# Two more weight slots, a two-expert loop and one block less around the expert stage of a two-layer-type transformer kernel

## The chip, the cores and the metric

The kernel runs on one NeuronCore of a Trainium2 chip. The metric is the device time of one execution in microseconds (us), median of several runs; lower is better.

## The reference, cut to what matters

`reference()` is a first block (one layer: a hybrid mixer, then a mixture of experts) followed by a second block (two layers of sparse and latent attention with a feed-forward part). The change touches the mixture of experts of the first block and the seams at its two ends:

```
def first_block(...):
    ...
    x = x + g1[:, None, :] * y                       # out1: the mixer's output projection
    h = rms_norm(x, norm2_g[l]) * (1.0 + sc2[:, None, :]) + sh2[:, None, :]
    y = moe(h, router_w[l], router_b[l], exp_w_up[l], exp_b_up[l], exp_w_down[l], exp_b_down[l])
    x = x + g2[:, None, :] * y
    ...
```

`moe` sends each of the 512 token rows to 4 of 32 experts, computes up = h @ exp_w_up + b_up, a clamped gate times a linear part, and that @ exp_w_down + b_down, weighted by the gate. All data are float32. The weights of one expert are 8 MB (up) and 4 MB (down).

## The kernel before, in words

The program is a row of stages. A stage is a *block*: each engine gets its own code, and the engines meet at the block's end. The stages here are, in order, the output projection with the routing in its tail (`out1_stage`, class `Routing`), the expert stage (`expert_stage`), and the projection of the second block.

**Weights.** An expert's weights come as 12 chunks of 1 MB (`CHUNKS`, 8 of them `UPS`). `LENT` = 22 places ("slots") in SBUF are lent to them, in turn: chunk number s (12 for each expert) lies in slot s mod 22. The pattern of slots repeats after `CYCLE` = 22 / gcd(12, 22) = 11 experts. SyncE (SP) issues every chunk, in order. In `out1_stage.loads` it issues the first 22: four before the projection's own weights, the rest when the projection is over, some of them behind a wait on a step of the routing that still uses their place. In the expert stage it waits in `load` (L2710) for the last use of the chunk that lay in the slot (`up_done`, `down_done`, L2720 to L2723), and then for the landing of the chunk four before (L2639), so that about four are under way.

**Rows.** Rows are sorted by expert into 85 groups ("row blocks") of 32, two to five for each expert. For each row block GpSimd (POOL) gathers rows with an indirect DMA (L2759) and scatters results (L2767); VectorE (DVE) transposes and scales the gathered rows (L2887, L2892, L2894), adds the bias (L2899), clamps, and multiplies; ScalarE (ACT) does the sigmoid (L2865); TensorE (PE) runs the up chunks of a row block (L2800) and then the down chunks of the row block before it (L2809). `run` is the first row block of an expert, `rest` a loop on the engine over its others.

**Loops.** PE's outer loop (L2851) holds 11 experts and runs twice, with the other experts in straight code; SP's (L2730) too. DVE's loop holds one expert, ACT's and POOL's one row block.

**Biases.** An expert's two bias rows (8 KB and 4 KB) go to `moe_bias_row`. SP issues them (L2700, L2702) in the middle of the chunks of the same expert, behind a wait on `bias_spread`, and DVE spreads them over the partitions (L2880) in the expert's first row block.

**The seam.** Between `out1_stage` and `expert_stage` all engines meet; L270 is the end of the first block. `run_idle` (L475) is a row of matmuls without use at the start of the expert stage, nine of them.

Of the kernel before, what the change touches and what calls it, by code (L numbers as in the profile page):

```python
# [254 lines left out]
def split_gemm_stage(k, name, jobs, banks=8, last_key=None, norm=None, beside=None, ready=None, wave=1, turns=0, tails=None, halved=None, loads=None, gain=None, inner=None, split_ahead=False):  # L255
# [14 lines left out]
    with ExitStack() as ctx:  # L270
# [10 lines left out]
        aside = beside and beside(ctx, evac_done)  # L281
        block = ctx.enter_context(nc.Block())
        for tail in behind:
            if tail.gpsimd:
                block.gpsimd(tail.gpsimd)
        if aside:
            block.gpsimd(aside.gpsimd)
# [6 lines left out]
        @block.sync  # L294
        def _(sp):
            if loads:
                loads(sp, behind, aside)
            else:
                if aside:
                    aside.sync(sp)  # L300
                load_chunks(k, sp, last_key)

        @block.tensor
        def _(pe):
# [73 lines left out]
            for tail in behind:  # L378
                tail.tensor_end(pe)

# [39 lines left out]
        def _(act):  # L420
# [13 lines left out]
            work(act, "act", split)  # L434

        @block.vector
        def _(dve):
# [10 lines left out]
            work(dve, "dve", split)  # L448

# [1711 lines left out]
def part1(k, a, mod_dram, h2_dram, x_dram):  # L2161
    nc = k.nc
    narrow = [P, 2, 2, ND * NARROW]
    with ExitStack() as ctx:
# [46 lines left out]
        k.expert_small, k.expert_words = tok_at + 5 * 4 * half, (w2_at - tok_at) // 4 + 8 * half  # L2211
        k.expert_w2 = nc.alloc_sbuf_tensor_at("expert_w2", [P, 8 * half], F32, offset=w2_at)
        k.split_at = w2_at + 1408
        with split_hT(k, "hT_out1"):
# [4 lines left out]
            with nc.sbuf_tensor("out1_w", narrow, F32R) as k.w_split, nc.sbuf_tensor("gated", [P, NARROW], F32) as k.gated:  # L2219
                out1_stage(k, a, tok_at, h2_dram, x_dram)  # L2220

def out1_stage(k, a, at, h2_dram, x_dram):
# [18 lines left out]
    def loads(sp, behind, aside):  # L2246
# [17 lines left out]
        load(16)  # L2264
        sp.wait_ge(routing.parted, NT)
        load(17)
        sp.wait_ge(routing.stored, 16 * NT)
        for s in (18, 19):
            load(s)
# [3 lines left out]
        load(20)  # L2273
        sp.wait_ge(routing.place_listed, 1)
        load(21)

    split_gemm_stage(k, "out1", jobs, banks=3, turns=5, tails=tails, loads=loads)


class Routing:  # L2280
# [8 lines left out]
    def __init__(self, k, ctx, at, job_bank, bank, evac_done, rank, final, h2_dram, x_dram):  # L2289
# [43 lines left out]
        self.list_bank = [b[:, 0:LISTS] for b in bank[0:2]]  # L2333
        self.squared, self.rooted, self.inverted, self.scaled, self.turned, self.taken_act, self.taken_dve = (
# [122 lines left out]
    def place(self, dve):  # L2457
# [36 lines left out]
        dve.wait_ge(self.gates_listed, 1)  # L2494
        nc.vector.tensor_copy(k.row_gate[:, 1:], self.list_bank[1])

# [7 lines left out]
    def gpsimd(self, pool):  # L2504
        k, ops = self.k, self.k.nc.gpsimd
        pool.wait_ge(self.started, 1)
        ops.tensor_scalar(k.first[:, 0:NE], self.start[0:1, :], 1.0 / BR, None, ALU.mult)
        ops.tensor_scalar(k.first[:, NE:NE + 1], self.ends[0:1, NE - 1:], 1.0 / BR, None, ALU.mult)
        ops.tensor_scalar(k.first[:, NE + 1:], self.ends[0:1, NE - 1:], 1.0 / BR, -1.0, ALU.mult, ALU.add)
# [104 lines left out]
LENT = 22  # L2614
# [25 lines left out]


def expert_stage(k, a, h2_dram, x_dram):

    nc = k.nc
    quarter = [slice(BR * q, BR * q + BR) for q in range(PARTS)]
    DOWNS, UPW = CHUNKS - UPS, 2 * YCOLS
    with ExitStack() as ctx:
        def sem(s):  # L2650
            return nc.alloc_semaphore(f"moe_{s}")

        def sb(s, shape, dt=F32):
            return ctx.enter_context(nc.sbuf_tensor(f"moe_{s}", shape, dt))

        def ps(s):
            return ctx.enter_context(nc.psum_tensor(f"moe_{s}", [P, COL], F32))

        chunk = [[k.expert_chunk(c, r) for c in range(CHUNKS)] for r in range(CYCLE)]
        loaded = k.expert_loaded  # L2660

        work = k.mod[:, 0:2, :].rearrange("p a (b n) -> p (a b) n", n=2 * P)
        rows, y, rowsT, hidT, sig, hid = (work[:, n, :] for n in range(6))
# [1129 lines left out]
```

## Time and profile before

| | |
|---|---|
| median of 3 runs | 2735.29 us (2733.44 to 2738.8) |
| the profiled execution's own time | 2732.22 us |
| its span, first to last instruction | 2730.4 us |
| PE, DVE, ACT, POOL busy | 94%, 50%, 28%, 11% of the span |
| mean DMA rate | 217 GB/s |
| mean DMA rate from 440 to 1370 us | 414 GB/s |

All times inside the span are us from its start. The expert stage lies between about 385 and 1400 us. The shares are averages over stages with different limits: what bounds the expert stage has to be read inside that window.

### The profile page before, as it was taken

What the parts mean: (1) busy time and instruction counts of PE and PEld (TensorE: products, weight loads), DVE (VectorE), ACT (ScalarE), POOL (GpSimd) and SP (SyncE); (2) the same over time, 40 slices, a digit from 0 to 9 for tenths busy, and PEclk for the clock granted to TensorE, in tenths of its full rate; (3) what the DMA queues carried; (4) which work ended last, traced back from release to release, by engine and by line L of the source; (5) the groups of instructions that cost most, each with busy time, mean ns of one, the idle gap of its engine ahead of it and who ended that gap; (6) DMA issues with size and microseconds to landing.
All of it is one profiled execution on the core that took longest, in us unless ns stands there. A gap on an engine that the chain in (4) does not pass through costs nothing. (4 is left out here: it accounts for less than half of the span.)

```text
span 2730.4 us, 56367 instructions
## 1 busy us (share of the span) xinstructions
PE 2562.3 (94%) x21559; PEld 1724.4 (63%) x21560; DVE 1356.8 (50%) x3120; ACT 755.2 (28%) x1652; POOL 299.6 (11%) x448
## 2 busy tenths in 40 slices
PE   6999989899889879999979999999999999999998
PEld 6986864344333324443448667888888766888887
DVE  3238744354434334544465785533345686544343
ACT  4236420000000000000023575422234267423322
POOL 3112002122222112222210000000000000000000
PEclk8999989999999999999989999999999999999999
DMA  7354289999999999999984201222223310122231
GB/s 231 114 191 154 78 326 379 420 419 417 417 403 420 420 417 417 379 419 419 418 285 140 94 2 39 93 93 100 93 93 104 107 44 9 62 93 101 94 107 47
DMA packets 171856, 591.15 MB, mean 217 GB/s; under 512 B 28334, under 2 KB 55790, under 8 KB 122488
## 3 DMA queue, kind: packets, MB, share of 16 engines
q1 hardware_dynamic: 159120, 565.80, 52.9%
q0 software_dynamic: 10160, 18.02, 2.0%
q10 hardware_dynamic: 2360, 4.29, 0.4%
q8 instruction: 155, 2.54, 0.4%
q14 instruction: 61, 0.50, 0.1%
HBM read 576.35 MB, written 17.45 MB: 217 GB/s over the span
## 5 line engine op out<-in xcount | busy, mean ns | idle before, releaser
L2800 PE MATMUL moe_up<-expert_w,mod 128*32 128x512 f32 x3456 | 423.8, 612 | 49.7 <-DMA expert_w<-in_exp_w_up 26.4
L2800 PEld LDWEIGHTS moe_up<-expert_w,mod 128*32 128x32 f32 x3456 | 119.7, 112 | 299.8 <-issue 222.4
L2865 ACT ACTIVATE mod<-mod 128x256 f32<-128x256 f32 x85 | 35.5, 417 | 955.7 <-DVE mod L2901 945.8
L429 ACT ACTIVATE feed_w<-ring 128x1024 fp32r<-128x1024 f32 (+1 forms) x160 | 153.8, 1035 | 263.5 <-PE feed_bank L376 263.5
L2809 PE MATMUL moe_down<-expert_w,mod 128*32 128x256 f32 x3424 | 207.9, 384 | 1.7 <-DVE mod L2912 1.7
L2800 PE MATMUL moe_up<-ring,mod 128*32 128x512 f32 x1504 | 186.1, 607 | 23.4 <-DMA ring<-in_exp_w_up 13.6
L374 PE MATMUL feed_bank<-feed_w,mlp_u_hi 128*128 128x512 f32 x512 | 199.7, 390 | 0.0
L376 PE MATMUL feed_bank<-feed_w,mlp_u_lo 128*128 128x512 f32 x512 | 199.5, 390 | 0.0
L375 PE MATMUL feed_bank<-feed_w,mlp_u_hi 128*128 128x512 f32 x512 | 199.5, 390 | 0.0
L443 DVE TENSOR_TENSOR feed_w<-ring,feed_w 128x1024 fp32r<-128x1024 f32 (+1 forms) x160 | 185.4, 1221 | 13.2 <-ACT feed_w L429 12.9
L2809 PEld LDWEIGHTS moe_down<-expert_w,mod 128*32 128x32 f32 x3424 | 121.8, 112 | 92.4 <-issue 33.8
L374 PE MATMUL feed_bank<-feed_hT_hi,feed_w 128*128 128x512 f32 x448 | 174.6, 390 | 0.0
L375 PE MATMUL feed_bank<-feed_hT_lo,feed_w 128*128 128x512 f32 x448 | 174.6, 390 | 0.0
L376 PE MATMUL feed_bank<-feed_hT_hi,feed_w 128*128 128x512 f32 x448 | 174.5, 390 | 0.0
L2136 DVE TENSOR_TENSOR x<-x,feed_bank 128x512 f32<-128x512 f32 x80 | 54.9, 687 | 229.6 <-PE feed_bank L376 229.6
L2899 DVE TENSOR_TENSOR mod<-moe_up,mod 128x512 f32<-128x512 f32 x85 | 58.0, 682 | 177.9 <-PE moe_up L2800 177.9
L3522 DVE TENSOR_TENSOR mlp_relu<-mlp_relu 128x512 f32<-128x512 f32 x64 | 44.3, 692 | 187.3 <-ACT mlp_u_hi L3519 187.3
L2800 PEld LDWEIGHTS moe_up<-ring,mod 128*32 128x32 f32 x1504 | 50.3, 111 | 132.7 <-issue 88.3
L2767 POOL DMA_INDIRECT expert_rows<-mod,moe_place x85 | 88.5, 1041 | 286.2 <-DVE mod L2922 281.7
L2887 DVE STREAM_TRANSPOSE moe_rows_turn<-mod 128x256 f32<-128x256 f32 x86 | 55.7, 648 | 111.6 <-DMA mod<-h_rows,moe_index 85.8
L1179 ACT ACTIVATE att_p<-att_p,att_neg 128x512 f32<-128x512 f32 (+3 forms) x192 | 105.3, 551 | 12.6 <-DVE att_neg L1224 12.3
L374 PEld LDWEIGHTS feed_bank<-feed_w,mlp_u_hi 128*128 128x128 f32 x512 | 96.2, 188 | 19.9
(560 smaller groups left out, 5021.6 us busy)
## 6 DMA issues: line engine op xcount, KB each, us to landing
expert_w<-in_exp_w_up SPq DMA_DIRECT2D x163, 1024.0 KB, 10.4
expert_w<-in_exp_w_down SPq DMA_DIRECT2D x81, 1024.0 KB, 10.2
ring<-in_exp_w_up SPq DMA_DIRECT2D x70, 1024.0 KB, 10.4
ring<-in_w_ff SPq DMA_DIRECT2D x32, 2048.0 KB, 8.8
ring<-in_exp_w_down SPq DMA_DIRECT2D x36, 1024.0 KB, 10.2
x<-in_exp_w_up SPq DMA_DIRECT2D x23, 1024.0 KB, 10.5
ring<-in_ada_w SPq DMA_DIRECT2D x11, 2048.0 KB, 11.0
ring<-in_w_in SPq DMA_DIRECT2D x6, 2048.0 KB, 8.3
```

The lines of the kernel that those rows point to most:

```text
L374: nc.tensor.matmul(out, lhsT.hi, rhs.hi, start=(i == 0), stop=False)
L375: nc.tensor.matmul(out, lhsT.hi, rhs.lo, start=False, stop=False)
L376: mm = nc.tensor.matmul(out, lhsT.lo, rhs.hi, start=False, stop=last)
L429: hi = nc.scalar.activation(halves.hi[:, at], w[:, at], ACT.Copy)
L443: lo = nc.vector.tensor_tensor(halves.lo[:, at], w[:, at], halves.hi[:, at].bitcast(F32), ALU.subtract)
L1179: nc.scalar.activation(p[:, b, m, 0:nk], p[:, b, m, 0:nk], ACT.Exp, bias=neg[:, b, m:m + 1], scale=-1.0, accum_out=total[:, n % 4, m:m + 1 ...
L2136: return nc.vector.tensor_tensor(k.x[:, t, cols], k.x[:, t, cols], psum, ALU.add)
L2767: pool.indirect_dma_start(y_parts, bass.IndirectOffsetOnAxis(ap=place[:], axis=0), y, None, bounds_check=NO_PLACE - 1, oob_is_err=False).t ...
L2800: mm = nc.tensor.matmul(up[quarter[q], :], rowsT[:, c, :], w[:, q], start=(c == 0), stop=(c == UPS - 1))
L2809: mm = nc.tensor.matmul(down[quarter[q], 0:YCOLS], hidT[:, 2 * at + h, :], w[:, h, q * YCOLS:(q + 1) * YCOLS], start=(at == 0 and h == 0), ...
L2887: nc.vector.transpose(turned_by_part, rows_by_run).then_inc(rows_turned, 1)
L2899: nc.vector.tensor_tensor(pre, up[:], bias_up, ALU.add).then_inc(up_taken, 1)
```

## The change

- The scratch that the chip keeps for dynamic transfers is set to 2048 bytes of a partition (it was not set before, so the default held). The room goes to `expert_w4`, two more slots: `LENT` = 24, and with it `CYCLE` = 2. `expert_chunk` maps the slots anew.
- The loops of PE and SP over experts hold 2 experts and run 15 times.
- `expert_stage` becomes the class `Experts`, whose engine code is appended to the block of the output projection through a new parameter `after` of `split_gemm_stage`. The block end between them is gone. In its place each engine waits for `first_made`, three small results of POOL. The accumulators are two of the projection's banks.
- Five chunks, not four, are issued ahead of the projection's own weights, and the waits on the routing's steps stand before other chunks.
- ACT issues the biases of expert e + 1 after those of expert e are spread; SP issues none.
- `run_idle` runs 6 matmuls, not 9. DVE zeroes `moe_bias_row` before it waits for the first gathered rows, copies the gate rows after that, and transposes the second rows before the first bias.

```diff
-def split_gemm_stage(..., split_ahead=False):
+def split_gemm_stage(..., split_ahead=False, after=None):
...
+        follower = after and after(behind[0])
         block = ctx.enter_context(nc.Block())
...
+            if follower:
+                follower.sync(sp)
...
             for tail in behind:
                 tail.tensor_end(pe)
+            if follower:
+                follower.tensor(pe)
...
-        for s in range(4):
+        for s in range(5):
             load(s)
         load_chunks(k, sp, keys[-1])
         sp.wait_ge(k.groups_done, k.last_group[k.chunk_no[keys[-1]]])
-        for s in range(4, 16):
+        for s in range(5, 17):
             load(s)
...
-LENT = 22
+LENT = 24
 CYCLE = LENT // math.gcd(CHUNKS, LENT)
...
-            def load(e, r, c0=0):
-                begin, end = first_block(sp, e - 1), first_block(sp, e)
-                for c in range(c0, CHUNKS):
-                    if c == LENT - CHUNKS:
-
-                        sp.wait_ge(bias_spread, e * 2)
-                        load_bias(sp, e)
+            def load(e, r):
+                begin = first_block(sp, e - 1)
+                for c in range(CHUNKS):
                     old = (c + CHUNKS - LENT) % CHUNKS
-                    last = begin if c < LENT - CHUNKS else end
+                    last = begin
...
-            load(1, 1, LENT - CHUNKS)
-            with sp.Fori(0, NE // CYCLE) as i:
+            with sp.Fori(0, (NE - 2) // CYCLE) as i:
                 for r in range(2, CYCLE + 2):
                     load(i * CYCLE + r, r)
-            for r in range(2, NE % CYCLE):
-                load(NE // CYCLE * CYCLE + r, r)
...
-            run_idle(k, down, 9)
+            run_idle(k, down, 6)
...
+            def next_bias(e):
+
+                act.wait_ge(bias_spread, e * 2 + 2)
+                load_bias(act, e + 1)
+
             load_bias(act, 0)
             open_gate(0)
-            with act.Fori(1, first_block(act, NE)) as b:
-                open_gate(b)
+            next_bias(0)
+            rest(0)
+            with act.Fori(1, NE - 1) as e:
+                open_gate(first_block(act, e))
+                next_bias(e)
+                rest(e)
...
-    nc = bacc.Bacc("TRN2", target_bir_lowering=False, num_devices=1)
+    nc = bacc.Bacc("TRN2", target_bir_lowering=False, num_devices=1, dynamic_dma_scratch_size=2048)
```

The order of instructions shows the seam. First SP's chunks in the output projection's block; `ring`, `x` and the `expert_w` tiles are slots. Before:

```order
L2639 DMA x<-in_exp_w_up 128x2048
L2639 DMA expert_w_51<-in_exp_w_up 128x2048 x3
L2639 DMA x<-in_exp_w_down 128x2048
L2639 DMA expert_w_50<-in_exp_w_down 128x2048
L270 UNCONDITIONAL_BRANCH
L2708 UNCONDITIONAL_BRANCH
L2706 TENSOR_LOAD first_block
L2706 ISA x2
```

After:

```order
L3002 DMA x<-in_exp_w_up 128x2048 x2
L3002 DMA expert_w_51<-in_exp_w_up 128x2048
L3002 DMA expert_w_51<-in_exp_w_down 128x2048 x2
L3002 DMA expert_w_50<-in_exp_w_down 128x2048
L3002 DMA expert_w_4043<-in_exp_w_down 128x2048
L2321 UNCONDITIONAL_BRANCH
```

Two more chunks stand ahead of the loop, which follows with no block end between.

Next DVE at the seam: `row_place` and `row_from` are the routing's last results, `moe_rows_turn` the transposed rows, `mod` holds the stage's small tiles. Before:

```order
L2493 TENSOR_SCALAR row_from<-row_place 128x126
L2495 COPY row_gate<-out_turn 128x126
L270 UNCONDITIONAL_BRANCH
L2876 UNCONDITIONAL_BRANCH
L2887 STREAM_TRANSPOSE moe_rows_turn<-mod 128x256
L2892 TENSOR_TENSOR mod<-moe_rows_turn,row_affine 128x256
L2894 TENSOR_TENSOR mod<-mod,row_affine 128x256
L2939 MEMSET moe_bias_row 128x768
L2940 MEMSET mod 128x256
L2942 COPY mod<-mod 32x256 x4
L2880 STREAM_SHUFFLE mod<-moe_bias_row 128x512
L2887 STREAM_TRANSPOSE moe_rows_turn<-mod 128x256
```

After:

```order
L2859 TENSOR_SCALAR row_from<-row_place 128x126
L2556 MEMSET moe_bias_row 128x768
L2495 STREAM_TRANSPOSE moe_rows_turn<-mod 128x256
L2500 TENSOR_TENSOR mod<-moe_rows_turn,row_affine 128x256
L2502 TENSOR_TENSOR mod<-mod,row_affine 128x256
L2562 COPY row_gate<-out_turn 128x126
L2563 MEMSET mod 128x256
L2565 COPY mod<-mod 32x256 x4
L2495 STREAM_TRANSPOSE moe_rows_turn<-mod 128x256
L2488 STREAM_SHUFFLE mod<-moe_bias_row 128x512
```

The second transpose now stands before the bias, not behind it.

Last PE around the loop's jump back. These rows close the loop of the changed kernel (L2428 is the inner loop over an expert's other row blocks, L2442 the outer one over two experts; `out_turn` and `out_bank` are the accumulators):

```order
L2400 MATMUL out_bank<-expert_w_4042,mod 32x256 x32
L2428 REGISTER_ALU
L2428 COMPARE_AND_BRANCH
L2442 REGISTER_ALU
L2442 COMPARE_AND_BRANCH
```

Before, the same two compare rows of the outer loop stand after the code of 11 experts; now after that of two.

## Rows read from the trace of the kernel before

**Rows 1.** The page: PE and DMA, busy tenths in 40 slices.
```profile
PE   6999989899889879999979999999999999999998
...
DMA  7354289999999999999984201222223310122231
```

**Rows 2.** Waits of SP's queue from 420 to 1370: us in total, times, longest.
```profile
SPq L2639 <- DMA expert_w<-in_exp_w_up: 276.0, 144, 3.9
...
SPq L2723 <- PE moe_up L2800: 23.7, 11, 9.7
```

**Rows 3.** Windows: length, PE, PEld, DVE, ACT, POOL busy, PEclk, DMA share, GB/s.
```profile
362.00:1379.00 1017.00, 927.48 (x11054) 395.01 (x11057) 454.12 (x1108) 44.96 (x110) 220.32 (x340) 0.96 1.00 411
...
410.00:420.00 10.00, 10.00 (x128) 4.04 (x124) 4.71 (x11) 0.42 (x1) 2.36 (x4) 1.00 0.40 145
770.00:776.00 6.00, 5.01 (x32) 1.32 (x36) 0.00 (x0) 0.00 (x0) 1.24 (x2) 0.63 0.72 261
1110.00:1122.00 12.00, 12.00 (x148) 4.69 (x144) 4.72 (x11) 0.42 (x1) 3.50 (x5) 1.00 0.52 197
```

**Rows 4.** Timeline at the seam: start us, us, engine, line, operation.
```profile
382.34 1.15 POOL L2514 DMA_INDIRECT mod<-h_rows,moe_index  x1 [0.89 <-POOL moe_index L2511]
...
386.40 3.60 SPq L2639 DMA_DIRECT2D expert_w<-in_exp_w_down  x1
390.62 0.65 DVE L2887 STREAM_TRANSPOSE moe_rows_turn<-mod 128x256 f32<-128x256 f32 x1 [4.47 <-PEq L270]
...
390.74 4.18 PE L475 MATMUL moe_down<-ident 128*128 128x128 f32 x18 [4.91 <-PEq L270]
...
394.84 1.42 PE L2800 MATMUL moe_up<-ring,mod 128*32 128x512 f32 x8
```

**Rows 5.** Timeline of the first row blocks.
```profile
402.46 1.01 POOL L2759 DMA_INDIRECT mod<-h_rows,moe_index  x1 [0.86 <-POOL moe_index L2756]
...
404.61 2.47 PE L2800 MATMUL moe_up<-ring,mod 128*32 128x512 f32 x16 [2.34 <-DVE mod L2894]
...
408.66 0.65 DVE L2887 STREAM_TRANSPOSE moe_rows_turn<-mod 128x256 f32<-128x256 f32 x1 [2.26 <-DMA mod<-h_rows,moe_index]
...
417.83 1.20 SPq L2639 DMA_DIRECT2D ring<-in_exp_w_down  x2
```

**Rows 6.** Timeline of SP and PE where their 11-expert loops jump back.
```profile
764.75 0.33 SPq L2639 DMA_DIRECT2D ring<-in_exp_w_down  x1
...
766.38 1.94 PE L2800 MATMUL moe_up<-expert_w,mod 128*32 128x512 f32 x8 [6.00 <-issue]
770.99 4.49 PE L2800 MATMUL moe_up<-expert_w,mod 128*32 128x512 f32 x24 [2.67 <-issue]
...
772.48 1.03 SPq L2639 DMA_DIRECT2D expert_w<-in_exp_w_up  x2
...
778.74 1.90 PE L2809 MATMUL moe_down<-expert_w,mod 128*32 128x256 f32 x32
```

**Rows 7.** Windows of one and of three passes of PE's inner loop.
```profile
1095.81:1126.80 30.99, 30.99 (x392) 12.52 (x384) 14.30 (x33) 1.25 (x3) 7.68 (x13) 1.00 0.82 334
1085.68:1096.00 10.32, 10.32 (x128) 4.20 (x132) 5.73 (x15) 0.42 (x1) 3.17 (x5) 1.00 1.01 416
```

**Rows 8.** DMA queues from 440 to 1370: packets, MB; then all queues from 1091 to 1129.
```profile
q8 instruction: 64, 1.05, 0.5%
q14 instruction: 17, 0.14, 0.0%
...
q1 hardware_dynamic: 1719, 12.37, 79.4%
q0 software_dynamic: 386, 0.93, 6.5%
```

**Rows 9.** Timeline of PE behind a late DVE, and at the stage's end.
```profile
1346.77 1.50 PE L2800 MATMUL moe_up<-expert_w,mod 128*32 128x512 f32 x12 [1.23 <-DVE mod L2894]
...
1390.41 3.66 PE L2809 MATMUL moe_down<-expert_w,mod 128*32 128x256 f32 x64 [1.71 <-DVE mod L2912]
```

More of the change, by code:

```diff
@@ L252, in split_chunk, with split_gemm_stage @@
     return Halves(at[:, 0], at[:, 1])
-def split_gemm_stage(k, name, jobs, banks=8, last_key=None, norm=None, beside=None, ready=None, wave=1, turns=0, tails=None, halved=None, loads=None, gain=None, inner=None, split_ahead=False):
+def split_gemm_stage(k, name, jobs, banks=8, last_key=None, norm=None, beside=None, ready=None, wave=1, turns=0, tails=None, halved=None, loads=None, gain=None, inner=None, split_ahead=False, after=None):
     nc = k.nc
@@ L281, in split_gemm_stage, with _ @@
         aside = beside and beside(ctx, evac_done)
+        follower = after and after(behind[0])
         block = ctx.enter_context(nc.Block())
         for tail in behind:
-            if tail.gpsimd:
+            if tail.gpsimd and not follower:
                 block.gpsimd(tail.gpsimd)
+        if follower:
+            @block.gpsimd
+            def _(pool):
+                behind[0].gpsimd(pool)
+                follower.gpsimd(pool)
         if aside:
@@ L2272, in loads @@
         sp.wait_ge(routing.gates_listed, 1)
-        load(20)
+        load(18)
+        sp.wait_ge(routing.parted, NT)
+        load(19)
+        sp.wait_ge(routing.stored, 16 * NT)
+        for s in (20, 21):
+            load(s)
         sp.wait_ge(routing.place_listed, 1)
-        load(21)
-    split_gemm_stage(k, "out1", jobs, banks=3, turns=5, tails=tails, loads=loads)
+        for s in (22, 23):
+            load(s)
+    split_gemm_stage(k, "out1", jobs, banks=3, turns=5, tails=tails, loads=loads, after=lambda routing: Experts(k, a, h2_dram, x_dram, routing))
 class Routing:
@@ L2506, in gpsimd @@
         pool.wait_ge(self.started, 1)
-        ops.tensor_scalar(k.first[:, 0:NE], self.start[0:1, :], 1.0 / BR, None, ALU.mult)
-        ops.tensor_scalar(k.first[:, NE:NE + 1], self.ends[0:1, NE - 1:], 1.0 / BR, None, ALU.mult)
-        ops.tensor_scalar(k.first[:, NE + 1:], self.ends[0:1, NE - 1:], 1.0 / BR, -1.0, ALU.mult, ALU.add)
+        ops.tensor_scalar(k.first[:, 0:NE], self.start[0:1, :], 1.0 / BR, None, ALU.mult).then_inc(self.first_made, 1)
+        ops.tensor_scalar(k.first[:, NE:NE + 1], self.ends[0:1, NE - 1:], 1.0 / BR, None, ALU.mult).then_inc(self.first_made, 1)
+        ops.tensor_scalar(k.first[:, NE + 1:], self.ends[0:1, NE - 1:], 1.0 / BR, -1.0, ALU.mult, ALU.add).then_inc(self.first_made, 1)
         pool.wait_ge(self.place_listed, 1)
@@ L3654, in expert_chunk @@
         second, third = (first + 1) % SLOTS, (first + 2) % SLOTS
-        homes = [(self.ring, 2 * second + 1), (self.ring, 2 * third + 1)] + [(self.expert_w1, i) for i in (0, 1)]
-        homes += [(self.ring, 2 * second), (self.ring, 2 * third)] + [(self.expert_w2, i) for i in (4, 5, 6, 7)]
-        homes += [(self.ring, 2 * first + 1), (self.ring, 2 * first)] + [(self.expert_w2, i) for i in range(4)]
-        homes += [(x, 0)] + [(self.expert_w1, i) for i in (2, 3, 4)] + [(x, 1), (self.expert_w3, 0)]
+        homes = [(self.ring, 2 * second + 1), (self.ring, 2 * third + 1)] + [(self.expert_w1, i) for i in (0, 1)] + [(self.expert_w4, 1)]
+        homes += [(self.ring, 2 * first + 1), (self.ring, 2 * first)] + [(self.expert_w2, i) for i in range(5)]
+        homes += [(self.ring, 2 * second), (self.ring, 2 * third)] + [(self.expert_w2, i) for i in (5, 6, 7)]
+        homes += [(x, 0), (x, 1)] + [(self.expert_w1, i) for i in (2, 3, 4)] + [(self.expert_w3, 0), (self.expert_w4, 0)]
         home, i = homes[n]
```

543 lines of the change are left out of this document (279 added, 264 removed).

## The prediction

> **What bounds the kernel now.** I read first the page's slices: from the sixth slice (of 68 us each) to the twenty-first the DMA row stands at 8 or 9 while PE drops to 7 and 8 in places, and after it DMA is at 0 to 4 [rows 1]. So the expert stage alone is a matter of transfers. Next the windows over the stream of chunks: from 362, where SP issues chunk 4, to 1379 DMA has a share of 1.00 at 411 GB/s, and PE is busy 927 of 1017 us [rows 3]. SP's waits say the same: SP mostly waits for a chunk four before to land, and only 23.7 us for PE to free an up chunk's slot [rows 2]. A chunk (380 of them in that stretch) takes (1017 - 13.5) / 380 = 2.64 us, 31.7 us for an expert. PE takes 10.3 us for a row block [rows 7], so 85 / 32 x 10.3 = 27.4 us for a mean expert. The stream leads by a little, and an expert with four or five row blocks turns this round for a while.
>
> The stream has three holes [rows 3]: 410 to 420 (share 0.40, 6.0 us idle), 770 to 776 (0.72, 1.7 us) and 1110 to 1122 (0.52, 5.8 us). Together 13.5 us; by their GB/s against 419 they are 15.2 us. The first: all 22 slots are full and the next chunk is issued at 417.83, when PE's third row block has begun [rows 5]. The second is not a wait on data: PE sits idle 6.00 us and again 2.67 us for "issue", and SP issues nothing from 764.75 to 772.48, both where their loops of 11 experts jump back [rows 6]. In the third PE is busy all 12 us: an expert of five row blocks holds every slot.
>
> **Slots and the early chunk.** Two more slots are 2 x 2.64 = 5.3 us of stream. They cover 5.3 of the first 6.0 us and, when PE again holds everything, 5.3 of the third 5.8 us. I let 0.5 us stay in the third and 1 us in the first. The fifth chunk ahead of the projection's weights is sent into a stretch where DMA has room (the fifth slice, at 2 tenths), so 2.6 us leave the later stream. The slots are full that much sooner, which only helps because the first free slot also comes sooner (the seam, next).
>
> **The seam.** The last chunk before the seam holds SP until 386.40 + 3.60 = 390.0, and all engines start after it: DVE at 390.62, PE at 390.74 [rows 4]. PE then runs 4.18 us of idle matmuls and starts row block 0 at 394.84. Without the meeting DVE is bound by the gather issued at 382.34. A gather issued at 402.46 is waited for until 408.66 [rows 5], 6.2 us, so this one lands near 388.5. Transpose and two scalings (0.65 + 0.43 + 0.42) end near 390.2; the 6 idle matmuls (2.8 us) can run right after the routing's last lists and end by 389. PE starts near 390.3: 4.5 us earlier. Row block 1 started at 404.61 behind DVE [rows 5]; DVE transposed its rows behind the first bias. Now the transpose comes first and the bias is asked for earlier. With rows turned at 389.2 the second gather is issued near 390.7 and lands near 397, scaled behind block 0's sum near 400, again some 4.5 us earlier. The first slot comes free near 413, not at 417.8, while 24 slots are full at about 413: the 1 us of the hole's rest. PE's start at 390.3 is taken between two bounds: 394.8 (nothing gained) and 389.7 (gather as soon as 388).
>
> **Sum for the stream.** 13.5 (holes) + 2.6 (early chunk) - 0.5 - 1.0 (rests of the third and the first hole) = 14.6 us earlier.
>
> **Biases.** SP loses two issues an expert, DVE the wait for a late bias. In the stream's stretches that is worth nothing, since PE waits for a chunk anyway. Towards the end PE is busy without a pause, and there a late bias makes rows late: PE waits 1.23 us at 1346.77 [rows 9], and one case like it near 1283. I take 2 us, bounds 0 and 3. ACT waits on `bias_spread` with the next sigmoids queued behind it, but DVE gives that before it asks for the next one, and ACT is busy 45 of 1017 us [rows 3]: nothing. The bytes are the same.
>
> **The end of the stage.** After the last chunk (about 1379) PE works until 1390.41 + 3.66 = 1394.1 [rows 9]. Counted from chunk 7 of the last expert, which lands four chunks before the last one, PE still has 3.7 us of downs, one row block (10.3), the wait for the hidden rows (1.7) and the last downs (3.7): 20 us against 10.6 + 15.1 = 25.7 now. So PE can come 14.6 + 2 = 16.6 us earlier without being held by the stream. What follows moves along.
>
> **Scratch and loops when all goes well.** The scratch is 2048 bytes of a partition. Only POOL's transfers use it, and POOL has at most a gather and a scatter of 32 rows under way; its busy time is 220 of 1017 us [rows 3]. I cost it at nothing; if each gather went up by 1 us, PE's row block of 10.3 us would still cover the chain of gather (6.2) and DVE (about 3). The loops of two experts jump back 14 times instead of once. In the good case a jump costs nothing and the 1.7 us of the second hole go (they are in the sum).
>
> Does a jump cost something? This is the largest question. PE's code comes in packets of 16 KB (64 packets, 1.05 MB [rows 8]) at two for an expert. An expert's code is two row blocks of 256 matmul and weight-load instructions and a few others, so a packet holds about 256. The inner loop, over 256 instructions, lies in two packets at least, with the next one fetched ahead. From 1091 to 1129 PE goes through it again and again (392 and 384 in three passes [rows 7]), and the instruction queue moves nothing [rows 8]: PE keeps at least three packets and jumps back for nothing. The new outer loop is about 1070 instructions, 5 or 6 packets with one ahead: seven at most. The trace does not show whether they stay. SP's loop of 24 chunks is about 135 instructions at 128 to its 8 KB packet: two packets, one ahead.
>
> By the Trainium skill (Runtime: NRT & Kernel Launch, section Instruction fetch mechanics) instruction memory is only two lines of 16 KiB, a taken branch out of that window stalls, and kernels therefore prefer unrolled code. By this rule even the inner loop with its fetch ahead would stall, and the trace disagrees: no packet, no stall. The same section gives TensorE 128 KiB and the others 32 KiB, 2048 and 512 instructions, by which both new loops stay; no run here shows that yet.
>
> **Forecast.** Against the execution of 2732.2 us: 2732.2 - 16.6 = 2715.6. Against the median that is shown, 2735.3 - 16.6 = 2718.7; I say 2718. Its own range is 2711 (holes by their GB/s, biases 3) to 2724 (PE's start gains half). Chance 0.64.
>
> **Rival A, slower: PE fetches at each jump back.** Speaks for it: that is just what happened at 766, and the new loop is four times the inner one. Price of a jump: at 766.38 PE had been idle 6.00 us, and from there to the downs at 778.74 it took 12.4 us for what takes 6.7, the clock at 0.63 of full (the lower of its two levels, 1.2 of 2.4 GHz, for most of it, after the idle stretch) [rows 3, 6]: 6.0 + 5.7 - 1 of ordinary change of expert = 10.7 us. PE becomes the bound: 390.3 + 85 x 10.3 + 32 x 0.5 + 14 x 10.7 + 4 (first row blocks) = 1436 against 1394. +42 us, less what overlaps: 2777. It decides from about 6 us a jump: there PE's sum passes today's end. Chance 0.15.
>
> **Rival B, slower by a little: only SP fetches.** Each jump holds the stream 1.7 us as at 770: 14 x 1.7 = 23.8 us on the stream, -14.6 + 23.8 = +9.2, with the biases +7 to +9: 2743. For it: SP's stall at 764.75 to 772.48. Against it: its new loop is far shorter. Chance 0.10.
>
> **Rival C: less comes through.** The first row blocks don't start sooner (the gather is slower among 18 MB of queued chunks) and PE, not the stream, holds from the middle on; only the slots count: 5 to 10 us, 2725 to 2731. Chance 0.11.
>
> **How the numbers follow.** 0.2% (5.5 us) is about what a measurement of this kernel can tell from no change. The range 2711 to 2744 holds the forecast, B and C but for their edges, and leaves out A: about 0.8. Faster by over 0.2%: 0.64 and most of C, 0.72. Slower: A and most of B, 0.23. Within: 0.05.
>
> **What would show it.** Right: the window 410 to 420 at a DMA share near 1; PE's first expert matmul near 390; no packets of the instruction queues and no idle for "issue" in PE at every second expert; DVE's wait for the bias gone; last downs ending near 1377. Wrong: idle of 5 us or more for "issue" every 60 us (A), pauses in SP's issues without a wait (B), or gathers over 7 us (C, and the scratch).

## The result and the profile after

| | median | lowest to highest |
|---|---|---|
| before, 4 runs | 2735.85 us | 2733.44 to 2738.8 |
| after, 4 runs | 2714.82 us | 2713.86 to 2715.44 |

The ratio is 0.9924, 95% interval 0.9911 to 0.9938: 21.0 us less. The forecast was 2718.0 in a range of 2711 to 2744. The profiled execution of after took 2715.44 us with a span of 2713.6; its own difference to that of before is 16.8 us.

The page of after shows PE, the DMA row and the instruction queues:

```profile
PE   6998989899989889999979999999999999999998
...
DMA  7454279999999999999973201222223300122221
...
q8 instruction: 94, 1.54, 0.2%
q14 instruction: 45, 0.37, 0.0%
```

At this grain the rows look like those of [rows 1]; only the instruction queues' bytes are visibly less. The windows that answer to [rows 3], with the same columns:

```profile
362.00:366.00 4.00, 3.74 (x45) 3.43 (x44) 3.12 (x15) 0.78 (x2) 0.00 (x0) 1.00 0.23 43
362.00:1362.00 1000.00, 928.47 (x11087) 413.54 (x11089) 458.47 (x1120) 44.96 (x110) 215.97 (x341) 0.97 1.01 416
410.00:420.00 10.00, 10.00 (x128) 3.98 (x124) 4.57 (x11) 0.37 (x1) 2.93 (x5) 1.00 1.02 424
770.00:776.00 6.00, 5.74 (x88) 2.79 (x79) 4.74 (x12) 0.42 (x1) 0.90 (x2) 1.00 1.02 421
1110.00:1122.00 12.00, 11.76 (x152) 5.05 (x147) 5.79 (x14) 0.42 (x1) 2.63 (x4) 1.00 1.01 425
```

All three holes are gone: 145, 261 and 197 GB/s have become 424, 421 and 425. The first window is new: at 362 to 366 the DMA share is 0.23, since in this execution SP resumed the chunks at 364.19, not at 362.

The timeline at the seam, which answers to [rows 4, 5]:

```profile
382.29 0.65 ACTq L2295 DMA_DIRECT2D moe_bias_row<-in_exp_b_up  x1
382.55 1.15 POOL L2877 DMA_INDIRECT mod<-h_rows,moe_index  x1 [0.89 <-POOL moe_index L2874]
...
388.38 2.93 PE L489 MATMUL out_bank<-ident 128*128 128x128 f32 x12
...
389.50 5.04 SPq L3002 DMA_DIRECT2D expert_w<-in_exp_w_down  x4
389.61 0.65 DVE L2495 STREAM_TRANSPOSE moe_rows_turn<-mod 128x256 f32<-128x256 f32 x1 [7.41 <-DMA mod<-h_rows,moe_index]
...
390.75 0.42 DVE L2502 TENSOR_TENSOR mod<-mod,row_affine 128x256 f32<-128x256 f32 x1
...
391.24 2.48 PE L2391 MATMUL out_turn<-ring,mod 128*32 128x512 f32 x16
...
401.12 1.48 PE L2391 MATMUL out_turn<-ring,mod 128*32 128x512 f32 x9 [2.25 <-DVE mod L2502]
```

DVE now waits for the gather (7.41 us), not for the meeting of the engines, and SP still issues chunks until 394.5 while PE has been at the first expert since 391.24. That is 3.6 us earlier than before; the second row block starts 3.5 us earlier, at 401.12.

The instruction queues from 440 to 1350, as in [rows 8], and PE's waits from 420 to 1365 (us in all, times, longest):

```profile
q8 instruction: 3, 0.05, 0.0%
q14 instruction: 1, 0.01, 0.0%
```

```profile
PE out_turn L2391 <- DMA expert_w<-in_exp_w_up: 30.0, 30, 1.8
PE out_turn L2391 <- issue: 12.1, 44, 0.3
```

PE fetched 63 packets of code in this window before, now 3, and none after 466. Both loops stay in their engines. "Issue" has no long piece any more (longest 0.3 us, 6.00 before), and PE never waits for DVE's scaled rows in this stretch, nor DVE for a bias. PE's end of the stage and the first matmul of the second layer:

```profile
1371.24 3.66 PE L2400 MATMUL out_bank<-expert_w,mod 128*32 128x256 f32 x64 [1.71 <-DVE mod L2533]
...
1389.52 1.97 PE L969 MATMUL in_turn<-ident,x 128*128 128x128 f32 x8 [14.62 <-DVE x L955]
```

The last downs end at 1374.9, 19.2 us earlier than in [rows 9]. The same first matmul of the second layer stood at 1409.14 in before. SP's last chunks of the stage, in before and in after:

```profile
1368.05 2.82 SPq L2639 DMA_DIRECT2D expert_w<-in_exp_w_down  x2
```

```profile
1346.81 7.87 SPq L3002 DMA_DIRECT2D expert_w<-in_exp_w_down  x4
```

The stream's last issue ends at 1354.68, not 1370.87: 16.2 us earlier. From there to the second layer's first matmul it takes 34.8 us, not 38.3.

**A clock for the stage.** Executions differ by some us in stages ahead of this one: over the fourteen profiles the first chunk after the projection's weights is issued between 361.7 and 373.9. So the experiments are read by two numbers. One is the median time by the ratio to before. The other is the *stage length* in the profile: from that issue to the first matmul of the second layer. It is 1409.14 - 362.01 = 1047.1 us before and 1389.52 - 364.19 = 1025.3 us after, 21.8 us less. The stage length has two pieces: the *stretch of the stream*, up to the end of SP's last chunk issue (1008.9 us before, 990.5 after, 18.4 less), and the *end of the stage* behind it (38.3 and 34.8, 3.4 less). Each stage length is one profile's, with whatever chance that execution had.

### The profile page after: what moved, and what is told of

Its sections match the earlier page's. It is cut to its first block and busy times, and to the rows that moved or that the text cites. A ratio compares the mean times of both kernels' runs of the same rounds, so it can differ in the third digit from the quotient of the medians.

```text
span 2713.6 us, 56970 instructions
## 1 busy us (share of the span) xinstructions
PE 2561.8 (94%) x21553; PEld 1741.0 (64%) x21554; DVE 1358.4 (50%) x3120; ACT 755.5 (28%) x1653; POOL 294.6 (11%) x448
## 5 line engine op out<-in xcount | busy, mean ns | idle before, releaser
L2391 PE MATMUL out_turn<-expert_w,mod 128*32 128x512 f32 x2720 | 336.3, 603 | 30.1 <-DMA expert_w<-in_exp_w_up 30.0
L2400 PE MATMUL out_bank<-expert_w,mod 128*32 128x256 f32 x5440 | 314.4, 382 | 1.7 <-DVE mod L2533 1.7
L2400 PEld LDWEIGHTS out_bank<-expert_w,mod 128*32 128x32 f32 x5440 | 204.6, 111 | 133.6 <-issue 52.2
L2391 PE MATMUL out_turn<-ring,mod 128*32 128x512 f32 x2112 | 261.1, 606 | 23.7 <-issue 12.1
L2391 PEld LDWEIGHTS out_turn<-expert_w,mod 128*32 128x32 f32 x2720 | 99.4, 110 | 234.1 <-issue 160.3
L2507 DVE TENSOR_TENSOR mod<-out_turn,mod 128x512 f32<-128x512 f32 x84 | 58.1, 692 | 373.9 <-PE out_turn L2391 373.9
L2391 PEld LDWEIGHTS out_turn<-ring,mod 128*32 128x32 f32 x2112 | 72.9, 110 | 158.2 <-issue 128.1
L2357 POOL DMA_INDIRECT expert_rows<-mod,moe_place x85 | 88.5, 1042 | 419.6 <-DVE mod L2543 387.4
L384 PEld LDWEIGHTS feed_bank<-feed_w,mlp_u_lo 128*128 128x128 f32 x512 | 96.1, 188 | 20.1
L382 PEld LDWEIGHTS feed_bank<-feed_w,mlp_u_hi 128*128 128x128 f32 x512 | 96.1, 188 | 19.8
L383 PEld LDWEIGHTS feed_bank<-feed_w,mlp_u_hi 128*128 128x128 f32 x512 | 96.1, 188 | 19.8
## 6 DMA issues: line engine op xcount, KB each, us to landing
expert_w<-in_exp_w_down SPq DMA_DIRECT2D x128, 1024.0 KB, 10.3
ring<-in_ada_w SPq DMA_DIRECT2D x11, 2048.0 KB, 10.9
```

What stands on the lines that cost most here:

```text
L382: nc.tensor.matmul(out, lhsT.hi, rhs.hi, start=(i == 0), stop=False)
L383: nc.tensor.matmul(out, lhsT.hi, rhs.lo, start=False, stop=False)
L384: mm = nc.tensor.matmul(out, lhsT.lo, rhs.hi, start=False, stop=last)
L2357: pool.indirect_dma_start(y_parts, bass.IndirectOffsetOnAxis(ap=place[:], axis=0), y, None, bounds_check=NO_PLACE - 1, oob_is_err=False).t ...
L2391: mm = nc.tensor.matmul(up[quarter[q], :], rowsT[:, c, :], w[:, q], start=(c == 0), stop=(c == UPS - 1))
L2400: mm = nc.tensor.matmul(down[quarter[q], 0:YCOLS], hidT[:, 2 * at + h, :], w[:, h, q * YCOLS:(q + 1) * YCOLS], start=(at == 0 and h == 0), ...
```

## The experiments

Each median is of 5 to 12 runs. "By the median" is the ratio's difference to 0.9924 (parts undone in the changed kernel) or to 1 (parts alone, and pairs), times 2735 us. The interval of after alone is 3.7 us to either side, so the ratios do not tell two changed kernels apart when they differ by under about 5 us.

### Parts undone in the changed kernel

**The block end back** (e1). The follower's engine code goes to a block of its own:

```diff
+        own.close()
         if follower:
-            follower.vector(dve)
+            block = ctx.enter_context(nc.Block())
+            block.sync(follower.sync)
+            ...
```

> The changed kernel with the block end put back between the projection and the expert stage; slots, loops, biases and idle matmuls stay. Changed kernel: 2714.8 us, PE's first expert matmul at 391.24. Theory (the seam is worth what it delays, and the delay is now longer, since SP issues chunks until 394.5 and nobody starts before it): PE starts near 398.5, the DMA hole at 410 to 420 comes back with 7 us, and the kernel takes 2722. Rival 1 (the start only moves back to where it was, 394.8): 2718.4. Rival 2 (24 slots cover the seam by themselves, the start doesn't matter): 2715. Rival 3 (the seam is the whole gain): 2735.

2718.76 us, ratio 0.9936 (0.9923 to 0.9949): +3.3 by the median, +5.8 in stage length. The interval overlaps that of after, but every run of e1 (2717.27 to 2719.78) was longer than every run of after (up to 2715.44). The timeline of e1:

```profile
389.71 3.45 SPq L3002 DMA_DIRECT2D expert_w<-in_exp_w_down  x4
...
393.90 2.90 PE L489 MATMUL out_bank<-ident 128*128 128x128 f32 x12 [5.25 <-PEq L455]
396.74 1.92 PE L2391 MATMUL out_turn<-ring,mod 128*32 128x512 f32 x16
```

Everyone waits for SP's last chunk as the theory said, and PE starts 5.5 us later, not 7; the time is that of the first rival (2718.4), whose start at 394.8 did not happen. The hole is back in part: e1's window from 410 to 420 is

```profile
410.00:420.00 10.00, 10.00 (x128) 4.08 (x124) 4.62 (x11) 0.42 (x1) 1.40 (x3) 0.98 0.66 269
```

3.4 us idle. With 24 slots a start that is 5.5 us later costs 3 to 6 us. Not all of that hole is the seam: in e1 the granted clock was lower while PE ran the second row block, 0.79 from 404 to 412, where after has 1.00, and the block took 8.6 us instead of 6.9. The same dip is in before, and in e10 it is not:

```profile
404.00:412.00 8.00, 7.39 (x56) 2.15 (x60) 2.94 (x8) 0.01 (x1) 1.41 (x3) 0.79 1.01 418
```

```profile
404.00:412.00 8.00, 7.70 (x80) 2.63 (x84) 3.75 (x10) 0.42 (x1) 0.28 (x2) 1.00 1.01 419
```

So up to 1.7 us of the first hole, in before and in e1, are a matter of the clock in that execution.

**22 slots in use** (e2). Chunk s waits for the use of chunk s - 22:

```diff
-                    old = (c + CHUNKS - LENT) % CHUNKS
-                    last = begin
+                    old = (c + CHUNKS - 22) % CHUNKS
+                    last = begin if c < 10 else end
```

> The changed kernel, but SP sends chunk s only when chunk s - 22 has been used, as if there were 22 slots; all else stays. Theory (slots are worth the stream's holes that they cover): a hole of about 7 us between 405 and 420, one of about 2 us near 1107 to 1115, stage and kernel 7 us later: 2722. Rival 1 (the early start of PE alone closes the holes): 2715. Rival 2 (nearly all of the gain is slots, since the stream is the bound and all its holes come back, 13.5 us): 2728.

2722.69 us, ratio 0.9955 (0.9939 to 0.9972): +8.5, stage +10.9. Two windows of e2, the columns as above:

```profile
410.00:420.00 10.00, 10.00 (x128) 4.03 (x124) 4.71 (x11) 0.42 (x1) 3.51 (x5) 1.00 0.44 155
1100.00:1122.00 22.00, 21.77 (x268) 10.20 (x264) 10.63 (x25) 0.84 (x2) 5.35 (x8) 1.00 0.71 285
```

5.6 us idle in the first, 6.4 in the second. The time is the theory's 2722. Its first hole was about right (7), the second was three times what it gave (2).

**Biases from SP again** (e3).

```diff
+                    if c == 10:
+                        sp.wait_ge(bias_spread, e * 2)
+                        load_bias(sp, e)
...
-                next_bias(e)
```

> The changed kernel, but SP issues the biases of an expert again, in the middle of the same expert's chunks behind the same wait as before the change. Theory: PE's stage ends 2 us later, since a late bias only costs where PE is busy without a pause: 2717. Rival 1 (by a reckoning with the faster stream PE holds more often, so a late bias costs 5 us): 2720. Rival 2 (it is worth nothing, PE waits for a chunk anyway): 2715. DVE's wait for the bias row should come back with over 150 us whatever the price.

2723.68 us, ratio 0.9959 (0.9945 to 0.9974): +9.6, stage +11.6. Waits of DVE, and of PE, from 420 to 1365 in e3:

```profile
DVE mod L2486 <- DMA moe_bias_row<-in_exp_b_down: 159.8, 19, 15.4
...
PE out_turn L2396 <- DVE mod L2500: 28.1, 9, 4.6
```

A late bias holds DVE up to 15.4 us, the next rows are scaled late, and PE waits nine times. Where that lands shows the window around the five row blocks, of e3 and then of after:

```profile
1095.00:1135.00 40.00, 39.46 (x499) 18.34 (x492) 19.54 (x47) 1.67 (x4) 9.05 (x15) 1.00 0.84 346
```

```profile
1095.00:1135.00 40.00, 39.46 (x492) 18.01 (x485) 18.74 (x46) 1.67 (x4) 10.16 (x16) 1.00 0.99 410
```

The hole is back with 6 us though the slots are all there: PE, held up on its way, gives them back too late. Of the 11.6 us of stage length 6.6 lie in the stretch of the stream and 5.0 in the end of the stage, which takes 39.9 us and not 34.8. Another way for SP's biases to cost time would be SP's own wait for `bias_spread`. It comes to 7.7 us in three waits from 420 to 1365, the longest 3.1, two of them (5.9 us) between 1100 and 1200; but no window of 10 us from 420 to 1100 or from 1120 to 1350 is below 391 GB/s, which is 0.7 us of stream, so those waits did not stop it. Theory and rivals were all too small.

**Loops of 10** (e4): `Fori` over 10 experts in PE and SP, three rounds.

> The changed kernel with loops of 10 experts in PE and SP (three rounds each) in place of 2 (15 rounds). Theory (small loops stay in the engines, long ones are fetched): over 60 PE packets between 440 and 1360 come back, PE idles for issue twice (6.0 and 2.7 us, 10.7 us in all with the slow clock), SP pauses twice, the stream loses 2 holes and about 1 MB of packets; kernel 2724 to 2727. Rival 1 (PE has slack at the jumps, only the stream's loss counts, 2 x 1.7 + 2.5 us): 2721. Rival 2 (loops are worth nothing): 2715.

2727.42 us, ratio 0.9968 (0.9955 to 0.9981): +12.0, stage +13.8, at the upper end of the theory's 2724 to 2727. PE in e4 at the second of its two jumps back:

```profile
1030.71 3.66 PE L2400 MATMUL out_bank<-expert_w,mod 128*32 128x256 f32 x64
1040.28 3.52 PE L2391 MATMUL out_turn<-ring,mod 128*32 128x512 f32 x15 [5.90 <-issue]
1044.85 0.62 PE L2391 MATMUL out_turn<-ring,mod 128*32 128x512 f32 x1 [1.06 <-issue]
1044.86 3.19 PE L2391 MATMUL out_turn<-expert_w,mod 128*32 128x512 f32 x24
...
1050.03 4.04 PE L2400 MATMUL out_bank<-expert_w,mod 128*32 128x256 f32 x64
```

From downs to downs 19.7 us pass instead of 10.3: a jump costs PE about 9.3 us, in 5.90 and 1.06 us of idle and in slower matmuls (15 take 3.52 us where 16 take 1.92 at the full clock; the granted clock was 0.50 from 1040 to 1042, the lower of its two levels, behind that idle stretch). That is nearly the price of the prediction's rival A, 10.7. From 440 to 1350 the code queue of PE moves 65 packets again. Of the 13.8 us of stage length 13.0 lie in the stretch of the stream, and three things account for 12.4 of them: 4.3 where SP's own loop jumps back (336 GB/s from 730 to 740, 324 from 1040 to 1050), 2.5 for the packets, and 5.6 by which the hole at the five row blocks is larger, since PE comes to it late.

The kernel before jumps back only once, at 766. A loop of 10 jumps twice, the second time at 1040, shortly ahead of the expert of five row blocks. So 12 us is the price of loops of 10, and more than what the loops of before cost.

**A PE loop of 4** (e5) and **an SP loop of 6** (e6), one engine at a time.

```diff
-            with pe.Fori(0, (NE - 1) // CYCLE) as i:
-                for r in range(1, CYCLE + 1):
-                    run(i * CYCLE + r, r)
+            with pe.Fori(0, (NE - 1) // 4) as i:
+                for r in range(1, 4 + 1):
+                    run(i * 4 + r, r)
```

> The changed kernel (2714.8 us) with a PE loop of 4 experts (seven rounds, then three experts in straight code; about 2140 instructions, 8 to 9 packets of 16 KB) in place of 2; SP's loop stays at 2. Theory (PE keeps the 5 to 6 packets of a loop of 2, but not 8 to 9): two packets an expert come back, and each of 6 jumps back costs PE 6 to 10.7 us; kernel 2724 to 2732, more than the loops of 10 (2727) if the jumps are what costs. Rival (PE keeps 8 to 9 packets too): 2715, no packets. If the packets return without idle time at the jumps, the fetching alone costs 1 MB of stream, 2.5 us: 2717.

> The changed kernel with an SP loop of 6 experts (five rounds, about 400 instructions, 3 to 4 packets of 8 KB) in place of 2; PE's loop stays at 2. Theory: this still stays in the engine, 2715 and no more of its packets. Rival (SP keeps only 2 packets, so it fetches at each of 4 jumps and the stream pauses 1.7 to 2 us each time): 2722, with about 3 SP packets a round.

e5: 2738.16 us, ratio 1.001 (0.9996 to 1.0023): +23.5 over the changed kernel, stage +21.4, and slower than any other here. e6: 2717.29 us, ratio 0.9937 (0.9921 to 0.9954): +3.6, stage +3.8; its interval overlaps that of after. The queues of e5 and of e6 from 440 to 1350, and PE's waits for issue in e5:

```profile
q8 instruction: 76, 1.25, 0.6%
...
q14 instruction: 1, 0.01, 0.0%
```

```profile
q14 instruction: 23, 0.19, 0.0%
q8 instruction: 3, 0.05, 0.0%
```

```profile
PE out_turn L2391 <- issue: 44.4, 35, 6.4
```

Both loops are fetched again in each round. PE keeps 5 to 6 packets (a loop of 2) and not a loop of 4 (2140 / 256 = 8.4 packets, so 9 at least): on this the theory held, though its 2724 to 2732 was too small. Its six jumps cost 56 us of PE at 9.3 each, and 21 to 23 us of time, under 4 a jump, so more than half was hidden in PE's waits for chunks. For SP the theory fell: about 400 instructions do not stay. At 976.95 SP stops in e6 and goes on at 983.33:

```profile
971.70 5.25 SPq L3002 DMA_DIRECT2D expert_w<-in_exp_w_down  x3
983.33 1.01 SPq L3002 DMA_DIRECT2D ring<-in_exp_w_up  x2
```

and the stream has a hole at three of the four jumps, one of them here:

```profile
978.00:988.00 10.00, 9.65 (x128) 4.05 (x124) 5.22 (x13) 0.42 (x1) 2.05 (x3) 1.00 0.75 293
```

**Four early chunks** (e7): `range(4)` and `range(4, 17)` in `loads`.

> The changed kernel with 4 instead of 5 chunks ahead of the projection's weights. Predicted step: the fifth takes 2.6 us from the later stream: 2717.4. Rival (the fifth only fills the slots sooner, since without it the stream would just be 2.6 us further from full at 410 to 420): 2715, no hole in either.

2715.15 us, ratio 0.9924 (0.9904 to 0.9944): no difference by the median, as its rival had it, though the stage is 1389.4 - 362.1 = 1027.3 us long, 2.0 more than after, near the 2.6 forecast. The stage length of after counts from 364.19, a resumption that came 2.1 us later. One profile of each can't tell whether that delay belongs to the fifth chunk or to the scatter ahead of the stage. Other profiles with five early chunks resume at 361.7 (e12), 362.4 (e2, e4) and 362.6 (e3), so the fifth chunk need not delay it. What the fifth chunk is worth stays open between 0 and 2 us.

### Parts alone, and in pairs

**The scratch alone** (e8), in the kernel before:

```diff
-    nc = bacc.Bacc("TRN2", target_bir_lowering=False, num_devices=1)
+    nc = bacc.Bacc("TRN2", target_bir_lowering=False, num_devices=1, dynamic_dma_scratch_size=2048)
```

> The kernel before with the scratch for dynamic transfers set to 2048 bytes and nothing else. Theory: nothing, the time of before (2735 to 2736), and gathers that land in the same time as before. Rival (a small scratch makes gathers and scatters wait for each other): gathers over 1 us slower and the kernel 2738 or more.

2733.96 us, ratio 1.0 (0.9986 to 1.0013), stage 1413.4 - 366.4 = 1047.0 us against 1047.1: nothing. Its gathers land after a median of 6.2 us, as long as the one of [rows 5] took to DVE's start.

**The biases alone** (e9), in the kernel before, with the changed kernel's `next_bias` and no biases from SP.

> The kernel before with one edit: ScalarE issues the biases of the next expert once this one's are spread, SP issues none. The undoing of this edit in the changed kernel cost 9 us, not 2. Theory (late biases made PE wait 23 us in all, each wait also holds the slots back, and that costs where the slots are full): 5 to 9 us faster than before, 2728, PE's waits for the scaled rows gone. Rival 1 (as predicted, 2 us): 2734. Rival 2 (the cost in the changed kernel came from SP's wait in a 24 slot order, not there before): 2736.

2733.32 us, ratio 0.9992 (0.9982 to 1.0001): -2.2, stage -4.3. By the median this is the prediction's 2 us and the first rival's time; the theory's 5 to 9 us did not come. The interval reaches up to no change at all, and the profiled execution was the slowest of the twelve (2742.77 us), so the figure is a weak one. Its stage length is shorter by 1.8 us in the stretch of the stream and 2.6 in the end of the stage.

**The loops alone** (e10): the changed kernel with block end, 22 slots, 4 early chunks and SP's biases. It still has the small edits, 6 idle matmuls and DVE's new order among them, and so have e11 and e12.

> The changed kernel with everything undone but the loops and the scratch: block end back, 22 slots in use, 4 early chunks, biases from SP. So it is close to the kernel before with loops of 2. Theory (the loops are worth what the loops of 10 cost, about 12 us, less what other waits now cover): 2726 to 2729. Rival 1 (they are worth only the stall at 770 and 1 MB of packets, 4 us): 2732. Rival 2 (nothing, because PE's jump had slack): 2736.

2736.63 us, ratio 1.0006 (0.9994 to 1.0018): no difference that the interval can tell (+1.6), as its second rival had it; stage -3.1.

**Loops and biases together** (e11): the same, but with the biases from ACT.

> The two parts on PE's side alone: the changed kernel's loops of 2 and its biases from ScalarE, with the block end back, 22 slots in use and 4 early chunks. Loops alone gave nothing against the kernel before, biases alone about -2 us. Theory (the stream that no longer stalls meets slots that PE still holds, so the loops' gain was given back in the hole near 1105 to 1115, which grew from 5.5 to 8.9 us; with punctual biases PE comes to the five row blocks sooner and the gain stays): 8 us faster than before, 2727, hole near 1110 of at most 7 us. Rival 1 (the two just add, 0 and -2): 2733. Rival 2 (the undoings in the changed kernel add, 3.3 and 8.5 us over 2714.8): 2726.6, which does not differ from the theory in time, only in the hole.

2726.49 us, ratio 0.9969 (0.9954 to 0.9985): -8.5, stage -9.5. Time and hole (6.2 us below) are the theory's, 2727 and at most 7; the time is also the second rival's. By the median the two parts give more together than apart (-2.2 and +1.6), but in stage length they nearly add: -4.3 and -3.1 against -9.5.

**Slots and seam together** (e12): 24 slots, 5 early chunks and no block end, but loops of 10 and biases from SP.

> The two parts on the stream's side alone: 24 slots, 5 early chunks and no block end, but loops of 10 in PE and SP and the biases from SP. Theory (slots and seam are worth most of their holes by themselves, about 9 us, as the stream is what bounds): 2727. Rival 1 (the undoings of loops and biases add up, 12.6 and 9 us over 2714.8): 2736, so that slots and seam are worth nothing while PE is held up by late biases and jumps. Rival 2 (nearly the whole gain is here): 2718.

2731.69 us, ratio 0.9983 (0.9970 to 0.9995): -4.6, stage -4.5. Halfway between the theory's 2727 and the first rival's 2736. But this is not the kernel before with slots and seam: its loops of 10 bring the second jump at 1040, which before has not, with 326 and 328 GB/s at the two jumps. Slots and seam with the loops of before were not tried, so they may be worth more than 4.6 us. The window around the five row blocks in e10, e11 and e12, each from its own trace:

```profile
1095.00:1135.00 40.00, 39.46 (x496) 18.46 (x492) 18.77 (x44) 1.67 (x4) 10.07 (x16) 1.00 0.78 320
```

```profile
1095.00:1135.00 40.00, 39.78 (x500) 18.55 (x492) 18.39 (x44) 1.67 (x4) 10.20 (x16) 1.00 0.86 354
```

```profile
1095.00:1135.00 40.00, 40.00 (x496) 19.14 (x491) 18.45 (x44) 1.25 (x3) 9.98 (x15) 1.00 0.83 339
```

The table turns such rates into what the stream lost against 419 GB/s, in us: (419 - rate) x length / 419. The first hole is taken from 405 to 435, the third from 1095 to 1135, so that both lie inside in every trace.

| | first hole | third hole | end of the stage | median against before | stage against before |
|---|---|---|---|---|---|
| before | 6.4 | 6.2 | 38.3 | | |
| e9 biases | 6.1 | 5.3 | 35.7 | -2.2 | -4.3 |
| e10 loops | 3.6 | 9.5 | 40.1 | +1.6 | -3.1 |
| e11 loops, biases | 5.3 | 6.2 | 35.6 | -8.5 | -9.5 |
| e12 slots, seam, early chunk, loops of 10 | 0 | 7.6 | 38.3 | -4.6 | -4.5 |
| e1 all but the seam | 4.7 | 1.9 | 35.8 | -17.5 | -16.0 |
| e2 all but slots | 6.2 | 6.9 | 35.1 | -12.3 | -10.9 |
| e3 all but biases | 1.5 | 7.0 | 39.9 | -11.2 | -10.2 |
| e4 all but loops (10 in place of 2) | 0 | 6.5 | 35.7 | -8.8 | -8.0 |
| e5 PE loop of 4 | 0 | 9.3 | 41.5 | +2.7 | -0.4 |
| after | 0 | 0.9 | 34.8 | -20.8 | -21.8 |

In e12 slots and seam do close the first hole by themselves. The stream then comes to the expert of five row blocks that much sooner, PE, behind its jump at 1040, does not, and the third hole is larger than in before. In e10 likewise: without the pause at 770 the third hole grows by 3.3 us, which gives back half of what the first hole (2.8, of which 1.7 are the clock at the second row block and not the loops), the pause (1.7) and the packets (2.5) had brought. Only where all parts are there is the third hole closed too; take out slots or biases, or put loops of 10 for those of 2, and it is back at 6 to 7 us (block end alone: 1.9).

The end of the stage goes by the biases: with SP's it takes 38.3 to 40.1 us, with ACT's 34.3 to 35.8 (e6 and e7 with 34.4 and 34.3 among them), but for e5, where PE lags. So the 3.4 us that it gives in after are in the main theirs.

The two pairs give 8.5 and 4.6 us, 13 in sum, and 21 together. Undoing one part at a time costs 3.3, 8.5, 9.6 and 12.0, which is 33 in all. The second jump of the loops of 10 is in the 4.6 and in the 12.0 and makes both gaps look larger than they are; by how much is not shown. Free of it are the biases, 2.2 us alone and 9.6 with all the rest changed (4.3 and 11.6 in stage length), and the third hole, which comes back when slots alone or biases alone are undone.

## Why the prediction was right, and where its steps were not

**What bounds, and the holes: right.** The stage's 21.8 us are the holes (6.4 + 6.2 - 0.9), the 1.7 us at 770, the 2.5 us that 1 MB of instruction packets took at 418 GB/s, 3.4 us at the stage's end, and 2 to 2.6 us of the fifth chunk: 21.3 to 21.9. The last figure is the one that e7 leaves open. Up to 1.7 us of the first hole were the clock in the profiled execution of before.

**The seam: right, a little large.** 3.6 us earlier instead of 4.5. The gather landed about 1 us later than reckoned (DVE's transpose at 389.61, forecast 388.5).

**The sum for the stream, 14.6 us: the size came, the way it was split did not.** With all parts in place the holes give 13.4 us (the 1.7 at 770 with them) where 12.0 were reckoned. But the sum counted slots, seam and early chunk by the holes that they cover, as if PE's pace behind the holes were given. Together, with SP's biases and loops of 10, they are worth 4.6 us by the median (e12). The "5.3 of the third 5.8 us" of two slots need a PE that arrives in time: in e12 that hole is 7.6 us, and with every part but the biases it is 7.0 (e3).

**Biases, 2 us with bounds of 0 and 3: mis-sized in company.** Alone they give 2.2 us by the median, with an interval that reaches up to no gain. The 2 us were put to the stage's end, and there they are: 2.6 us in e9, 3.4 in after. One of the two cases read for it was not one: the wait near 1283 is for a chunk, not for DVE. The sentence that failed is "In the stream's stretches that is worth nothing, since PE waits for a chunk anyway": In before PE's waits for late rows from 420 to 1365 are this row:

```profile
PE moe_up L2800 <- DVE mod L2894: 23.3, 14, 3.6
```

They were not idle time that PE would have had anyway. They put off the release of slots: SP's biases make the stretch of the stream 6.6 us longer in the changed kernel (e3) and 1.8 in before (e9). With the stage's end the cost is 2 to 4 us alone and 9.6 with everything else changed.

**Scratch: nothing, shown by e8.**

**The loops.** That the jumps of two experts cost nothing was right; no packet comes after 466 and no stall is left. Too small was what the old loops cost. The prediction took the stream's 1.7 us at 770 and left out the 9 us that PE lost there, as if PE could spare them. In the changed kernel PE cannot: with SP's loop untouched six jumps cost 21 to 23 us (e5), and loops of 10 in both engines 12.0 (e4). What PE's one jump cost in before is not shown by itself. The 1 MB of packets, 2.5 us of stream, was read in [rows 8] and left out of the sum.

**The sum.** Forecast -16.6 for the stage. Its own ends moved by 19.2 (last downs) and 21.8 (stage length), the median by 21.0. What was short are three terms: the packets of code (2.5 us, left out), the rests of the holes (1.4 us more came than was reckoned) and the end of the stage (3.4 us, not 2). The likeliest case's own range, 2711 to 2724, held the time partly by luck: its lower end was to be the holes by their GB/s (1.7 us more) and biases of 3 us (1 more), and that leads from 2718.7 to 2716.0, not to 2711; the measured 2714.8 lies below it, in room that no term had been given. (The 20 us that it reckoned from chunk 7 to the last downs add up to 19.4, which changes nothing.) What the parts give one another was not reckoned at all. The table and the traces suggest why they do: slots are a credit between two paces, and the third hole closes only when the stream's side and PE's side both have moved. That the row blocks of one expert decide it is read from the traces of these kernels; it wasn't tried with other row counts.

**Rival A** did not happen, but its mechanism and price are real (9.3 us of PE at a jump against 10.7; e4). Its sum let about 4 us a jump come through (42 over before and the 16.6 that would not be gained, 59 us of 14 x 10.7 = 150), and e5 has just under 4; the two jumps of e4 cost 6 to 7 each, with SP's pauses and the packets in it. The threshold "about 6 us a jump" does not follow from its own sum: 1286 + 14 x 6 = 1370, and today's end, 1394, is passed from 7.7 us on. **Rival B** as well: an SP loop that is fetched pauses for several us (e6). Its four jumps cost some 4 us in all, near 1 a jump and not 1.7. **Rival C** did not happen either: the start came 3.6 us sooner and gathers land in 6.0 us by the median. Its sign "gathers over 7 us" would have misled all the same, since the first gather took 7.06 us (382.55 to 389.61).

The Trainium skill (Runtime: NRT & Kernel Launch, section Instruction fetch mechanics) gives instruction memory as 128 KiB on TensorE and 32 KiB on most other engines. PE's loops agree with it: a loop of about 1070 instructions stays and one of about 2140 does not, between 6 and 9 packets of 16 KB. SP's loop of about 400 instructions, 26 KB, was fetched in each round, though by that figure it would stay. The same section's window of two pages, out of which a taken branch stalls, is contradicted by the changed kernel: 15 rounds of 5 to 6 packets with 3 packets fetched from 440 on.

## What to carry to other kernels

Where a stream fills slots and an engine empties them, don't price a part by the hole that it covers: ask which side is late at the next full buffer, and expect parts of both sides to give more together than alone. A part that gives little alone, as the biases here (2 us), may be worth 10 us once the rest has moved. When a part is undone by another value than the old one, as the loops of 10 here, count what that value brings of its own. Keep hardware loops of the busiest engine short enough that no packet of code is moved in steady state; the queue of instruction packets in the profile shows it at once.

## What was not expected of the hardware

- A PE loop of 4 experts is worse than one of 10: 2738 us against 2727. Nothing of it stays, and it jumps six times, not twice. At a jump three packets come one after the other (in e4 at 1036.6, 1042.4 and 1047.1), 5.8 and 4.7 us apart, and PE's 5.9 us of idle lie around the first.
- SP fetches a loop of some 400 instructions in every round (23 packets of 8 KB from 440 to 1350) and keeps one of 135.
- A scratch for dynamic transfers of 2048 bytes of a partition costs indirect gathers of 32 rows nothing.
